# Hybrid encoder block: depthwise convolution for even and odd tokens at once, its input and the gated product through memory

## The chip, the cores and the metric

The kernel runs on the 8 cores of one Trainium2 chip, one program on each with its own tokens. The time is device microseconds of the slowest core, the median of several runs.

## The reference

What one core computes, for 16,384 tokens of width 1024 in five sequences (one of 8192 tokens, four of 2048), in float32:

```python
h = rmsnorm(x, norm_g) * (1 + scale) + shift      # adaLN, per sequence
a_in, a_b, a_c, a_z, b_v, b_g, b_z = split(h @ w_in, 7 * [512])
y_a = a_b * dwconv3(a_c * a_in) * silu(a_z)
u   = b_v * sigmoid(b_g)
u   = dwconv31(u) + conv_b_b                       # per channel, centred, zero padding
y_b = silu(head_layernorm(u, ln_g, ln_b)) * silu(b_z)   # norm over groups of 64 channels
out = rmsnorm(x + gate * (concat(y_a, y_b) @ w_out), final_g)
```

## The kernel before, in words

Tokens go in 32 tiles of 512. Weights and activations of the matmuls are bfloat16, channels lie in partitions, tokens along the free dimension. One iteration i of the loop at L757 holds work of three tiles, in the order in which PE gets it:

- projections of tile i (`mm1`, matmuls at L521, blocks of 8 over the 1024 inputs): the GLU (`glu`, 64 matmuls, writes `u`), `t1_group` (64), `b2_b` (32, writes `gb`), `b2_a` (64, writes `ga`), 224 in all;
- `conv_phase` for tile i-1: the 31-tap convolution of `u` on PE (`conv_b`), with the head layer norm started in between;
- `stage_d` for tile i-2: 64 matmuls with `w_out`, the residual add (L714, DVE), square (L666, ACT), reciprocal root (L673, POOL), scaling (L678, DVE), store (L681).

The convolution reads the tile `X`, in which the 128 partitions are 4 taps x 32 channels: copies of `u`, each shifted by one token, made by `x_fill` (L587), 16 transfers from SBUF to SBUF. The weights `WC` are diagonal 128 x 32 blocks. Each of the 4 banks of 128 channels takes 8 steps `q` of 4 taps for 4 column strips `g` of 32 channels that run side by side in PE's array:

```python
bank[32 * g:32 * g + 32, :], lhsT=WC[:, j, g, q, :], rhs=X[:, j, g, 4 * q:4 * q + NT],
```

So there are 128 matmuls of 512 columns per tile at L595. Before each of them stands its weight load (PEld).

Layer norm of bank j: ACT copies the bank (L600), PE subtracts the group mean (`ln_center`, L605), ACT squares (L607), PE averages the squares (`ln_var`, L613), ACT takes Ln and Exp (L620, L622), DVE multiplies (L623); a whole iteration later ACT applies Silu (L630, `ln_out`) and POOL multiplies by `gb` into `yT` (L633). `conv_phase` puts centering and variance matmuls between the four convolutions; what is left goes as hooks behind the first three half banks of `stage_d`.

PSUM is eight banks of 512 columns, handed out by least recent use (`PB`, L247). The four convolution banks stay held until `ln_out`, so `stage_d` turns over four others. The row buffers `xb` are six (`XB`, L245). Every engine works off its instructions in the order written; a wait is in front of the instruction that needs it, and all that is behind it waits too. DMAs are issued by SP: at the start of an iteration the rows of tile i+1 (`a_load`, L308), after the GLU `x_fill`, after `t1_group` the transposes of the normalised rows (L331), then the rows for the residual (`d_loads`, L646), and the stores. POOL issues the loads of `w_in`. At the first tile of a sequence `fold_gate` multiplies `w_out` by the gate, in `X` and other tiles as staging (POOL, L473).

## Time and profile before

| | |
|---|---|
| median of 3 runs | 2375.08 us (2374.8 to 2375.59) |
| profiled execution, its own time | 2376.0 us |
| span of its slowest core (first to last instruction) | 2373.2 us |
| spans of the 8 cores | 2369.6 to 2373.2 us |
| mean granted TensorE clock | 0.990 to 0.997 of full |
| PE busy | 2322.2 us |
| DMA through the hardware queue | 340.49 MB, 53.1% of 16 engines' span |

The profile is of one execution on one core. The page gives busy time by engine, the chain of work that ended last, and groups of instructions by line. The trace behind it answers for shorter stretches: the chain of waits in order of time, the timeline of one engine, the busy time of all engines in chosen windows. A line number is one of the kernel before. A start is in us from the first instruction; in the timeline, brackets behind a row tell how long the engine had been idle before it and what released it.

### The profile page before, as it was taken

How to read it: one execution, taken by the hardware profiler on the slowest of the kernel's cores; microseconds unless marked ns; L12 is line 12 of the kernel's file. 1: busy time of each engine (PE TensorE's matmuls, PEld its weight loads, DVE VectorE, ACT ScalarE, POOL GpSimd, SP SyncE). 2: the span in 40 equal slices, each digit the busy share in tenths (PEclk: the TensorE clock that was granted, in tenths of full speed). 3: DMA queues.
4: the chain of work that ended last, by engine and by line, in shares of the span. 5: the costliest groups of instructions: out<-in, count | busy, mean ns of one | idle time of the engine just before them, and what ended most of it. 6: DMA issues, size and time to landing. Idle time of an engine off the chain costs nothing.

```text
span 2373.2 us, 42556 instructions; the slowest of 8 cores (2369.6 to 2373.2 us)
## 1 busy us (share of the span) xinstructions
PE 2322.2 (98%) x13766; PEld 1030.4 (43%) x13766; DVE 1225.3 (52%) x1967; ACT 1056.8 (45%) x1794; POOL 563.0 (24%) x514
## 2 busy tenths in 40 slices
PE   5999999999999999999999999999999999999997
PEld 1444444444444444444444444444444444444442
DVE  0245554554554555544555644555544554545547
ACT  1244345444354444354444354444454444454444
POOL 5114221211221211221211521215221242223203
PEclk9999999999999999999999999999999999999998
DMA  9945654445554445655446745456645655646444
GB/s 236 218 109 155 162 131 140 130 113 136 162 128 143 125 111 143 162 127 144 126 109 179 207 125 146 119 163 177 162 120 142 172 142 153 162 118 204 110 128 170
DMA packets 274565, 350.54 MB, mean 148 GB/s; under 512 B 144392, under 2 KB 217264, under 8 KB 273328
## 3 DMA queue, kind: packets, MB, share of 16 engines
q1 hardware_dynamic: 266736, 340.49, 53.1%
q0 software_dynamic: 7616, 7.34, 2.2%
q8 instruction: 118, 1.93, 0.3%
q14 instruction: 95, 0.78, 0.1%
HBM read 185.73 MB, written 67.13 MB: 107 GB/s over the span
## 4 chain that ended last, share of the span: by engine, by line
PE 96%; DMA 1%; SPq 1%; issue 1%; DVE 1%; POOL 0%; ACT 0%; POOLq 0%; DVEq 0%; ACTq 0%
PE pb L521 63%; PE pb L710 18%; PE pb L595 9%; PE pb L505 2%; PE pb L605 2%; PE pb L613 1%; DMA w_out_sb<-w_ada 1%; SPq L294 0%; DMA xb<-x 0%; SPq L349 0%; PE pb L358 0%; PE pb L486 0%; DVE xb L678 0%; POOL yT L633 0%; SPq L308 0%
## 5 line engine op out<-in xcount | busy, mean ns | idle before, releaser
L521 PE MATMUL pb<-hT,w_in_sb 128*128 128x512 bf16 x6944 | 1505.1, 379 | 0.6 <-PE pb L486 0.2
L521 PEld LDWEIGHTS pb<-hT,w_in_sb 128*128 128x128 bf16 x6944 | 679.3, 98 | 820.9 <-issue 3.1
L710 PE MATMUL pb<-w_out_sb,yT 128*128 128x512 bf16 x2048 | 462.0, 382 | 3.8 <-POOL yT L633 3.4
L673 POOL TENSOR_TENSOR rsE<-msE,mhalf 128x1 f32<-128x1 f32 x128 | 70.1, 548 | 1131.0 <-DVE msE L671 1128.9
L710 PEld LDWEIGHTS pb<-w_out_sb,yT 128*128 128x128 bf16 x2048 | 200.1, 98 | 246.1 <-issue 20.7
L553 DVE TENSOR_TENSOR t<-pb,tp 128x512 bf16<-128x512 f32 x128 | 88.9, 694 | 324.1 <-ACT xs L314 293.4
L576 DVE SCALAR_TENSOR_TENSOR tp<-t,caT_sb,tp 128x512 f32<-128x512 bf16 x256 | 230.1, 899 | 28.0 <-DVE tp L573 0.9
L623 DVE SCALAR_TENSOR_TENSOR pb<-pb,cbs,tp 128x512 f32<-128x512 f32 x128 | 96.8, 756 | 285.4 <-PE pb L613 216.2
L595 PE MATMUL pb<-X,WC 128*32 128x512 bf16 x4096 | 238.6, 380 | 0.0
L532 DVE SCALAR_TENSOR_TENSOR u<-tp,pb 128x512 bf16<-128x512 f32 x128 | 88.4, 691 | 273.7 <-PE pb L521 261.2
L633 POOL TENSOR_TENSOR yT<-tp,gb 128x512 bf16<-128x512 f32 x128 | 155.3, 1214 | 242.4 <-ACT tp L630 242.3
L530 ACT ACTIVATE tp<-pb 128x512 f32<-128x512 f32 x128 | 76.1, 597 | 303.5 <-PE pb L521 270.6
L559 ACT ACTIVATE tp<-pb 128x512 f32<-128x512 f32 x128 | 76.2, 597 | 303.4 <-PE pb L521 292.9
L551 ACT ACTIVATE tp<-pb 128x512 f32<-128x512 f32 x128 | 76.1, 597 | 252.4 <-PE pb L521 239.5
L714 DVE TENSOR_TENSOR xb<-pb,xb 128x512 f32<-128x512 f32 x248 | 169.8, 685 | 29.4 <-PE pb L710 25.5
L323 POOL TENSOR_SCALAR xs<-xb,rsA 128x1024 bf16<-128x1024 f32 x128 | 176.5, 1394 | 7.4 <-POOL rsA L320 5.3
L678 DVE SCALAR_TENSOR_TENSOR xb<-xb,rsE,fg_bc 128x1024 f32<-128x1024 f32 x124 | 164.7, 1328 | 5.0 <-POOL rsE L673 4.6
L666 ACT ACTIVATE tp<-xb 128x1024 bf16<-128x1024 f32 x124 | 131.1, 1057 | 70.8 <-DVE msE L671 57.2
L567 ACT ACTIVATE gb<-pb 128x512 bf16<-128x512 f32 x128 | 76.5, 598 | 179.4 <-PE pb L521 166.7
L595 PEld LDWEIGHTS pb<-X,WC 128*32 128x32 bf16 x4096 | 100.4, 96 | 125.1 <-issue 34.4
L600 ACT ACTIVATE sq<-pb 128x512 bf16<-128x512 f32 x128 | 75.8, 593 | 153.0 <-PE pb L595 150.5
L561 DVE TENSOR_TENSOR ga<-pb,tp 128x512 bf16<-128x512 f32 x128 | 87.7, 687 | 106.1 <-PE pb L521 98.0
(89 smaller groups left out, 1379.4 us busy)
## 6 DMA issues: line engine op xcount, KB each, us to landing
xb<-x SPq DMA_DIRECT2D x252, 512.0 KB, 8.2
X<-u SPq DMA_DIRECT2D x512, 135.0 KB, 2.9
y<-xb SPq DMA_DIRECT2D x124, 512.0 KB, 3.6
X<-w_out SPq DMA_DIRECT2D x20, 512.0 KB, 6.8
w_in_sb<-w_in POOLq DMA_DIRECT2D x28, 256.0 KB, 16.6
yT<-w_ada SPq DMA_DIRECT2D x6, 1024.0 KB, 10.9
w_out_sb<-w_ada SPq DMA_DIRECT2D x6, 1024.0 KB, 15.2
yT<-w_out SPq DMA_DIRECT2D x10, 512.0 KB, 7.7
```

The source lines that it names most:

```text
L323: T.op("gpsimd", lambda e, xbuf=xbuf, sub=sub: e.tensor_scalar(out=xs[:, sub, :], in0=xbuf[:], scalar1=rsA[:, sub:sub + 1], scalar2=1.0, o ...
L521: T.op("tensor", lambda e, bank=bank, kc=kc: e.matmul(bank[:], lhsT=w_in_sb[:, kc, col0:col0 + 128], rhs=hT[:, kc, :], start=(kc == 0), st ...
L532: T.op("vector", lambda e: e.scalar_tensor_tensor(out=u[:, j, 15:15 + NT], in0=th[:], scalar=1.0, in1=bank2[:], op0=ALU.add, op1=ALU.mult) ...
L553: T.op("vector", lambda e: e.tensor_tensor(out=t1[:, j, 1:1 + NT], in0=bank2[:], in1=ain[:], op=ALU.mult), reads=[akey, bkey2], writes=[(" ...
L576: T.op("vector", lambda e, k=k: e.scalar_tensor_tensor(out=acc[:], in0=t1[:, j, k:k + NT], scalar=caT[:, j * KA + k:j * KA + k + 1], in1=a ...
L595: T.op("tensor", lambda e, q=q, g=g: e.matmul(bank[32 * g:32 * g + 32, :], lhsT=WC[:, j, g, q, :], rhs=X[:, j, g, 4 * q:4 * q + NT], start ...
L623: T.op("vector", lambda e: e.scalar_tensor_tensor(out=bank[:], in0=bank[:], scalar=cbs[:, j:j + 1], in1=r[:], op0=ALU.add, op1=ALU.mult), ...
L633: T.op("gpsimd", lambda e: e.tensor_tensor(out=yT[:, 4 + j, :], in0=r[:], in1=gb[:, j, :], op=ALU.mult), reads=[rkey, ("gb", ti % 2, j)], ...
L666: T.op("scalar", lambda e: e.activation(out=jb[:].bitcast(BF16), in_=xbuf[:], func=AF.Square, accum_out=ssE[:, c:c + 1]), reads=xkeys, wri ...
L678: T.op("vector", lambda e: e.scalar_tensor_tensor(out=xbuf[:], in0=xbuf[:], scalar=rsE[:, c:c + 1], in1=fg_bc[:], op0=ALU.mult, op1=ALU.mult),
L710: T.op("tensor", lambda e, bank=bank, kc=kc, sub=sub, h=h: e.matmul(bank[:], lhsT=yT[:, kc, sub * 128:(sub + 1) * 128], rhs=w_out_sb[:, kc ...
L714: T.op("vector", lambda e, bank=bank, xbuf=xbuf, h=h: e.tensor_tensor(out=xbuf[:, h * NT:(h + 1) * NT], in0=bank[:], in1=xbuf[:, h * NT:(h ...
```

## The change

1. **Convolution.** `X` has 8 taps x 16 channels in its partitions, and `u` is split by parity of the token: 256 odd and 256 even ones. A weight block of 128 x 32 gives 16 channels for both parities. A matmul has 256 columns, 4 steps `q` suffice, and a bank holds two halves `hh` of 64 channels: 128 matmuls of 256 columns per tile. Columns of a bank that has channels x parity in partitions are tokens of one half, so bias and scale of squares, normalisation and Silu differ by half, and each of these becomes two instructions of 256 columns.
2. **Order.** `conv_phase` runs the four convolutions in one piece. Centerings, variances and the rest of the norm are hooks behind the first five half banks of `stage_d`.
3. **Input through memory.** `x_out` writes `u` to a scratch tensor in HBM (8 transfers), `x_in` reads `X` from it (8 transfers of 16 partitions, rows of 17,400 bytes).
4. **Gated product through memory.** The bank's layout differs from that of `gb` and `yT`. So `gb` goes out (`g_out`, 4 transfers) and comes back as `gbV` (`g_in`, 1), and POOL's product goes out (`y_out`, 1) and comes back as `yT` (`y_in`, 4).
5. **x rows by ACT's queue.** `a_load` and `d_loads` are issued by ACT; rows are every other token. `a_load` comes after the GLU, the squares of the rows go from `t1_group` to `b2_b`, the transposes behind `b2_b`, `d_loads` into `b2_a`.
6. `conv_a` has five DVE instructions in place of four. The last tile's `stage_d` takes the first half of the contraction for all eight half banks first. Constant matrices are built on DVE.

The diff, cut to its core:

```diff
-NQ = 8
+NQ = 4
+HN = NT // 2
+NG = 32
+PAD = 8
+UW = HN + 2 * PAD
+XN = NG * UW - 4
...
-        WC = sb("WC", [128, 4, 4, NQ, 32], BF16)
+        WC = sb("WC", [128, NG * NQ, 16, 2], BF16)
...
-        X = sb("X", [128, 4, 4, XW], BF16)
+        X = sb("X", [128, NG, UW], BF16)
...
-        gb2 = [sb("gb%d" % i, [128, 4, NT], BF16) for i in range(2)]
+        gb = sb("gb", [128, 4, NT], BF16)
+        gbV = sb("gbV", [128, 4, NT], BF16)
+        yV = gb
...
+        def rows(t, i, sub):
+
+            return t[i * NT:(i + 1) * NT, :].rearrange("(h p t) d -> t h p d", h=2, t=2)[1 - sub // 2, sub % 2]
+
+        def a_load(i, after=(), eng="scalar"):
             for sub in range(4):
                 xbuf, xkey = XB.next(pin=True)
-                T.dma("sync", lambda e, xbuf=xbuf, r=row0 + sub * 128: e.dma_start(out=xbuf[:], in_=x_d[r:r + 128, :]),
+                T.dma(eng, lambda e, xbuf=xbuf, sub=sub: e.dma_start(out=xbuf[:], in_=rows(x_d, i, sub)),
...
+        def g_out(i):
+
+            dst = gd[i % 2].rearrange("(c t) (j hh n) -> hh t c j n", t=2, j=4, hh=2)
+            T.dma_batch("sync", [lambda e, hh=hh, t=t: e.dma_start(out=dst[hh, t], in_=gb[64 * hh:64 * hh + 64, :, t * HN:(t + 1) * HN])
+                                 for hh in range(2) for t in range(2)], [("gb", j) for j in range(4)], [("gd", i % 2)], "st_g")
...
+        def y_out(i):
+            T.dma("sync", lambda e: e.dma_start(out=yd[i % 2], in_=yV[:].rearrange("p j n -> p (j n)")),
+                  reads=[("gb", j) for j in range(4)], writes=[("yd", i % 2)], semkey="st_y")
...
+        def x_out(i):
+
+            dst = ud[i % 2].rearrange("h c (j g l) -> h j g c l", j=4, g=8)
+            T.dma_batch("sync", [lambda e, h=h, j=j: e.dma_start(out=dst[h, j], in_=u_sb[i % 2][:, j, h, :]) for h in range(2) for j in range(4)],
+                        [("u", i % 2)], [("ud", i % 2)], "st_u")
...
+        def x_in(i):
+
+            Xf = X[:].rearrange("p g l -> p (g l)")
+            T.dma_batch("sync", [lambda e, w=w: e.dma_start(out=Xf[16 * w:16 * w + 16, 0:XN], in_=ud[i % 2, w % 2, :, (w + 1) // 2:(w + 1) // 2 + XN])
+                                 for w in range(8)], [("ud", i % 2)], Xkeys, "xfill")
 
         def conv_b(j):
             bank, bkey = PB.next(pin=True)
-            for q in range(NQ):
-                for g in range(4):
-                    T.op("tensor", lambda e, q=q, g=g: e.matmul(
-                        bank[32 * g:32 * g + 32, :], lhsT=WC[:, j, g, q, :], rhs=X[:, j, g, 4 * q:4 * q + NT],
-                        start=(q == 0), stop=(q == NQ - 1), tile_position=(0, 32 * g)),
-                        reads=[("WC", j)] + Xkeys, writes=[bkey], signal=(q == NQ - 1 and g == 3))
+            for hh in range(2):
+                for q in range(NQ):
+                    for g in range(4):
+                        G = 8 * j + 4 * hh + g
+                        T.op("tensor", lambda e, q=q, g=g, G=G, hh=hh: e.matmul(
+                            bank[32 * g:32 * g + 32, hh * HN:(hh + 1) * HN], lhsT=WC[:, G * NQ + q].rearrange("p c t -> p (c t)"),
+                            rhs=X[:, G, 4 * q:4 * q + HN], start=(hh == 0 and q == 0), stop=(hh == 1 and q == NQ - 1), tile_position=(0, 32 * g)),
+                            reads=["WC0", "WC1"] + Xkeys, writes=[bkey], signal=(hh == 1 and q == NQ - 1 and g == 3))
...
-            T.op("vector", lambda e: e.scalar_tensor_tensor(out=bank[:], in0=bank[:], scalar=cbs[:, j:j + 1], in1=r[:], op0=ALU.add, op1=ALU.mult),
-                 reads=[rkey, "cbs"], writes=[c["bkey"]])
+            for hh in range(2):
+                k, sl = 2 * j + hh, slice(hh * HN, (hh + 1) * HN)
+                T.op("vector", lambda e, k=k, sl=sl: e.scalar_tensor_tensor(out=bank[:, sl], in0=bank[:, sl], scalar=cbs[:, k:k + 1], in1=r[:, sl],
+                                                                            op0=ALU.add, op1=ALU.mult),
+                     reads=[rkey, "cbs"], writes=[c["bkey"]])
...
+            first = [half(n // 2, n % 2, (0, 1, 2, 3)) for n in range(8)] if i == ntiles - 1 else None
...
+            cs = [conv_b(j) for j in range(4)]
+
+            def norm(*steps):
+                def f():
+                    for fn, j in steps:
+                        fn(cs[j])
+                    if (ln_rstd, 3) in steps:
+                        table_of(AF.Silu, 1)
+                return f
+
             table_of(AF.Ln, 0)
...
+            return {0: norm((ln_center, 0), (ln_center, 1)),
+                    1: norm((ln_center, 2), (ln_var, 0), (ln_rstd, 0)),
+                    2: norm((ln_center, 3), (ln_var, 1), (ln_rstd, 1)),
+                    3: norm((ln_var, 2), (ln_rstd, 2)),
+                    4: norm((ln_var, 3), (ln_rstd, 3))}, (k, cs)
...
-            if 1 <= i < ntiles - 1:
-                a_load(i + 1)
...
+            if cur_ok:
+                u_halo(i)
+            if 1 <= i < ntiles:
+                x_out(i - 1)
+            if left is not None:
+                y_out(i - 2)
+            if 1 <= i < ntiles:
+                x_in(i - 1)
+            if left is not None:
+                y_in(i - 2)
             left = None
...
+            if 1 <= i <= ntiles:
+                g_in(i - 1)
+            if 1 <= i < ntiles - 1:
+                a_load(i + 1)
...
+                if i + 1 < ntiles:
+                    a_square(i + 1, j)
+            if cur_ok:
+                g_out(i)
+            if i + 1 < ntiles:
+                a_scale(i + 1)
+                if i > 0:
+                    a_transpose(i + 1)
...
+                if j == 2 and 2 <= i <= ntiles:
+                    d_loads(i - 2)
```

## Rows read from the trace of the kernel before

**Rows 1.** The page: header, and busy time of each engine with its share of the span.

```profile
span 2373.2 us, 42556 instructions; the slowest of 8 cores (2369.6 to 2373.2 us)
PE 2322.2 (98%) x13766; PEld 1030.4 (43%) x13766; DVE 1225.3 (52%) x1967; ACT 1056.8 (45%) x1794; POOL 563.0 (24%) x514
```

**Rows 2.** The chain that ended last: share by engine (page); its longest early piece.

```profile
PE 96%; DMA 1%; SPq 1%; issue 1%; DVE 1%; POOL 0%; ACT 0%; POOLq 0%; DVEq 0%; ACTq 0%
...
23.44 17.76 DMA w_out_sb<-w_ada
```

**Rows 3.** Chain of waits, one steady tile: start us, us, engine and line, instructions.

```profile
385.31 48.35 PE pb L521 x224
433.66 3.57 PE pb L595 x64
437.23 0.32 PE pb L605
...
444.03 0.22 PE pb L605
...
446.41 10.36 PE pb L710 x48
456.77 0.43 PE pb L521 x2
```

**Rows 4.** Windows of that tile: convolution, output, projection stage; busy us, instructions.

```profile
core 3: us, PE busy (x) PEld busy (x) DVE busy (x) ACT busy (x) POOL busy (x), PEclk, DMA share, GB/s
433.65:442.30 8.65, 8.65 (x135) 3.60 (x135) 3.27 (x9) 4.68 (x8) 0.00 (x0) 1.00 0.01 2
442.30:456.78 14.48, 14.48 (x69) 6.50 (x67) 9.61 (x15) 10.90 (x19) 1.09 (x2) 1.00 0.09 37
385.31:433.66 48.35, 48.35 (x229) 21.79 (x230) 25.00 (x38) 17.41 (x30) 12.31 (x11) 1.00 0.73 188
```

**Rows 5.** Windows: a stretch of the transposes of 128 columns.

```profile
100.95:101.34 0.39, 0.39 (x10) 0.39 (x8) 0.39 (x2) 0.00 (x0) 0.00 (x0) 1.00 1.06 305
```

**Rows 6.** Windows: centering after a wait, then the convolution's first instructions.

```profile
2319.81:2320.11 0.30, 0.30 (x1) 0.07 (x1) 0.00 (x0) 0.23 (x1) 0.30 (x2) 1.00 0.77 314
2320.11:2320.14 0.03, 0.03 (x5) 0.03 (x8) 0.00 (x0) 0.00 (x0) 0.03 (x1) 1.00 1.17 482
```

**Rows 7.** Groups by line: ACT and DVE of the layer norm and residual; busy, mean ns.

```profile
L607 ACT ACTIVATE sq<-pb,cbs 128x512 bf16<-128x512 f32 x128 | 87.4, 683 | 1.5 <-PE pb L613 0.3 <-PE pb L605 0.3
L600 ACT ACTIVATE sq<-pb 128x512 bf16<-128x512 f32 x128 | 75.8, 593 | 153.0 <-PE pb L595 150.5 <-PE pb L605 2.5
L622 ACT ACTIVATE tp<-tp 128x512 f32<-128x512 f32 x128 | 80.7, 630 | 11.7
L637 ACT ACT_TABLE_LOAD x64 | 82.1, 1283 | 1.1
L666 ACT ACTIVATE tp<-xb 128x1024 bf16<-128x1024 f32 x124 | 131.1, 1057 | 70.8 <-DVE msE L671 57.2 <-DVE xb L714 12.7
L714 DVE TENSOR_TENSOR xb<-pb,xb 128x512 f32<-128x512 f32 x248 | 169.8, 685 | 29.4 <-PE pb L710 25.5 <-DMA xb<-x 0.8
L623 DVE SCALAR_TENSOR_TENSOR pb<-pb,cbs,tp 128x512 f32<-128x512 f32 x128 | 96.8, 756 | 285.4 <-PE pb L613 216.2 <-ACT tp L622 69.2
```

**Rows 8.** SP's issues: timeline of the tile, landing (page), issue ns min/median/max (by line).

```profile
400.50 10.47 SPq L587 DMA_DIRECT2D X<-u  x16
...
xb<-x SPq DMA_DIRECT2D x252, 512.0 KB, 8.2
X<-u SPq DMA_DIRECT2D x512, 135.0 KB, 2.9
...
L646 SPq DMA_DIRECT2D xb<-x x124: 327/391/1673, 208.4 to 2325.1; - x124
```

**Rows 9.** The end: chain of waits, and PE's timeline with the idle time before it.

```profile
2323.23 7.64 DMA xb<-x
...
2331.80 0.38 PE L613 MATMUL pb<-sq,Bm 128*128 128x512 bf16 x1 [2.98 <-DVE xb L714]
```

More of the change, by code:

```diff
@@ L579, in conv_a @@
[L579 to L589 removed]
+            out, okey = TP.next()
@@ L703, in stage_d, with half @@
             yT = yT2[i % 2]
-            row0 = i * NT
+            def half(sub, h, kcs, bk=None):
+                bank, bkey = bk or PB.next(pin=kcs[-1] != 7)
+                for kc in kcs:
+                    T.op("tensor", lambda e, kc=kc: e.matmul(
+                        bank[:], lhsT=yT[:, kc, sub * 128:(sub + 1) * 128], rhs=w_out_sb[:, kc, h * NT:(h + 1) * NT],
+                        start=(kc == 0), stop=(kc == 7)),
+                        reads=[("yT", i % 2, kc), ("w_out", kc)], writes=[bkey], signal=(kc == kcs[-1]))
+                return bank, bkey
+            first = [half(n // 2, n % 2, (0, 1, 2, 3)) for n in range(8)] if i == ntiles - 1 else None
             for sub in range(4):
@@ L707, in stage_d @@
                 for h in range(2):
-                    bank, bkey = PB.next()
-                    for kc in range(8):
-                        T.op("tensor", lambda e, bank=bank, kc=kc, sub=sub, h=h: e.matmul(
-                            bank[:], lhsT=yT[:, kc, sub * 128:(sub + 1) * 128], rhs=w_out_sb[:, kc, h * NT:(h + 1) * NT],
-                            start=(kc == 0), stop=(kc == 7)),
-                            reads=[("yT", i % 2, kc), ("w_out", kc)], writes=[bkey], signal=(kc == 7))
+                    bank, bkey = half(sub, h, (0, 1, 2, 3, 4, 5, 6, 7)) if first is None else half(sub, h, (4, 5, 6, 7), first[sub * 2 + h])
                     T.op("vector", lambda e, bank=bank, xbuf=xbuf, h=h: e.tensor_tensor(
@@ L784, in build_nc @@
                 if ntiles > 1:
-                    a_load(1, [("w_in", 2, 7)])
+                    a_load(1, [("w_in", 2, 7)], "sync")
                 gate_loads([("w_in", 3, 7)])
@@ L823, in build_nc, with also @@
             if i == ntiles - 1:
-                x_fill(i)
+                x_out(i)
+                x_in(i)
             if i == ntiles:
-                hooks[1] = lambda f=hooks.get(1): (f(), conv_a(ntiles - 1, 2))
-                for j in range(4):
-                    hooks[3 + j] = lambda j=j: (ln_out(left[0], left[1][j]), conv_a(ntiles - 1, 3) if j == 1 else None)
+                def also(n, *fns):
+                    old = hooks.get(n, lambda: None)
+                    hooks[n] = lambda: [f() for f in (old,) + fns]
+                also(1, lambda: conv_a(ntiles - 1, 2))
+                also(3, lambda: conv_a(ntiles - 1, 3))
+                also(5, lambda: ln_out(left[0], left[1][0]), lambda: ln_out(left[0], left[1][1]))
+                also(6, lambda: ln_out(left[0], left[1][2]), lambda: ln_out(left[0], left[1][3]), lambda: y_out(ntiles - 1), lambda: y_in(ntiles - 1))
             if i >= 2:
```

261 lines of the change are left out of this document (118 added, 143 removed).

## The prediction

> **What bounds the kernel now.** I read the page first: PE is busy for 98% of the span, DVE, ACT and POOL for half of it or less [rows 1], and the chain that ended last is PE for 96% [rows 2]. So only what shortens or stalls PE's stream counts. The chain of waits over one steady tile shows that stream [rows 3]: it starts at 385.31 and again at 456.77, a period of 71.46 us, made of 224 projection matmuls (48.35), four convolutions of 32 matmuls, and 64 output matmuls with the layer-norm matmuls of 0.22 between them. There is no stall. The windows give 8.65 for the convolution stage, with three centerings and two variances in it, and 14.48 for the output stage with the other three [rows 4]. 30 such tiles have all stages.
>
> **The change, part by part.** Sums are against the profiled execution's own 2376.0 us (span 2373.2); the median of the three runs is 0.9 lower, so a gain is taken off 2375.1.
>
> *Convolution matmuls.* Still 128 per tile, in 32 rounds of four column strips, but with 256 columns in place of 512. Today a round takes 0.2159 (48.35/224 for one 512-column matmul; two convolutions, 16 rounds, take 3.57 with their switch) [rows 3]. Transposes of 128 columns run back to back: 7 weight loads begin in 0.39 (an eighth was in flight), 0.0556 a pair [rows 5]. On the line through both, 256 columns cost 0.109. So 32 rounds go from 6.91 to 3.49: 3.42 less per tile, if instructions come fast enough. That is the first unknown. A pair of weight load and matmul would have to issue each 27 ns; now it issues each 55.8 (3.57/64) [rows 3]. Ends: 27 ns (the array's own pace) and 55.8 (nothing gained). The nearest row is for the first: after PE had waited for ACT, 0.30 passed with only the centering matmul, and then 8 loads and 4 matmuls (a fifth, the centering, was in flight) began within 0.03 us [rows 6]. They had piled up while the array was busy with one matmul and a switch, so the queue can be ahead of the array. I take 3.49. The Trainium skill, "TensorE: Matmul & The Clock Gate", section Back-to-back issue gap, speaks against this: it gives about 81 ns per matmul of 128 columns in a stream of loads and matmuls. By it 128 pairs would take over 10 us and the change would lose; the transposes at 0.0556 with their loads contradict it here.
>
> *Mode switches.* A 128-row by 32-column convolution next to a full-array matmul costs extra: the centering in front of one takes 0.32 where it takes 0.22 in the output stage [rows 3], so 0.10 each. Today there are six edges per tile, afterwards two, all LN matmuls having moved into the output stage: 0.40 less.
>
> *Layer-norm order.* The eight matmuls stay (1.73). But their ACT work (four copies, table load, squares, Ln, Exp) now falls into 3.6 + 15.5 us instead of 8.65 + 14.5, and the squares, the DVE normalisation and the Silu are split in halves. Instruction cost: a 256-column half saves less than half; a 1024-column square takes 1.057 us and a 512-column copy 0.593 [rows 7], so some 0.91 ns a column and 0.13 us fixed. Eight more ACT instructions: about 1 us, where ACT is busy 33 of 71 [rows 4]. I worked through the stage with durations of [rows 7], from the first convolution matmul as 0. Copies end at 4.4, table load and its dummy at 5.9, squares 0 and 1 at 7.3, square 2 at 8.6, Ln and Exp of 0 at 10.0; the residual's square of sub 0 goes in front of hook 2's work and ends at 11.1; square 3 at 11.8; Exp of 1 at 13.2. DVE serves in order: normalisation 1 waits until 13.2, and behind it the residual add of bank 3 ends at 14.8. PE wants that bank again for its sixth half at 14.0. So a stall of 0.9 us per tile, new. Ends: 0 (if pipelining on ACT hides 0.9) and 2.
>
> *New period:* 48.35 + 3.49 + 0.10 + 13.82 + 1.73 + 0.9 = 68.4, that is 3.06 less. Times 30: 92.
>
> *Input of the convolution through memory.* The slot: x_fill starts at 400.50, the convolution at 433.66, so 33.2 us. Today 16 transfers take 10.47 to issue and 2.9 to land [rows 8]. Afterwards: 8 out (8 x 10.47/16 = 5.2, + 2.9), then 8 in. If these eight run at today's rate, 10.5 + 2.9: 21.5 in all. If at half the rate, since each lands in 16 partitions and today's in 32, 20.9 + 2.9: 31.9. Both fit, and I charge 0. Without the cover of the projections the whole 21.5 would show.
>
> *Gate and product through memory.* g_out, g_in, y_out, y_in: 10 more issues on SP, 8 x 0.65 + 2 x 0.39, 6.0 us, none in a hurry: y_in is needed in the output stage 33 us after the GLU. SP loses 8 loads of 0.39 and 8 net fill issues become 16 shorter ones: in balance it stays under half busy. Its order matters: x_in stands behind y_out, which waits for POOL's last product; POOL is busy 13.4 of 71 [rows 4], so that costs under 2 us of the slot's slack. In the five tiles that fold the gate POOL's w_out products come in between; slack again covers it. The DMA transposes move behind b2_b and end about when DVE starts hT; slack there is some 5 us, as PE has four banks free.
>
> *x rows by ACT's queue.* 8 issues of 0.39 [rows 8]: 3.1 us of ACT, in the projection stage where ACT is 17.4 of 48.35 busy [rows 4]. Their buffers were stored a stage earlier, so ACT should not wait. Queued behind them are the copies that free PE's banks, with eight banks in rotation: 0. The rows' squares move to b2_b: 1.06 + 0.59 per 1.73 of PE, so ACT keeps up, barely; 0.
>
> *conv_a:* one more DVE instruction each, 4 x 0.17; DVE is half busy: 0. *Setup* on DVE in place of POOL: hidden behind the 17.8 us in which PE's first work waits for weights [rows 2]: 0.
>
> *Tail.* In the last but one round today PE idles 2.98 for the residual rows, whose load hangs on a store, 7.64 [rows 9]. That chain does not shrink, so the last convolution's 3.4 is lost (I counted 30 tiles for it). Now ACT itself sits in that wait, with the convolution copies behind it; and the product's two trips to memory (about 3 each, the landing time in [rows 8]) are half covered by the 32 matmuls taken first (6.9). Ends 0 and 10; I take +4.
>
> Sum: 2375.1 - 92 + 4 = **2287**.
>
> **Rivals.**
> *No stall in the output stage.* ACT has 10.9 of 14.48 today without any [rows 4], and my 0.9 hangs on an order of 0.1 us steps. Then 30 x 3.96 = 119: 2375 - 119 + 0 to 4 = 2256 to 2260.
> *Issue-bound, slower.* Number of pairs is unchanged; if PE's sequencer can't deliver a pair faster than 55.8 ns, the convolution stays at 7.1, the switches give 0.4, the stall stays: 72.0 per tile, +0.6 x 30 + 4 = 2397. Place: PE, second half of each convolution stage. It decides from 51 ns a pair (6.5 us). Against it: [rows 6]. Values between give between.
> *The round trip comes late, slower.* At half rate it uses 31.9 of 33.2. If the four transfers of x rows (landing 8.2 [rows 8]) get served ahead of it, it lands 6.9 late: 75.3 per tile, +3.8 x 30 + 4: 2493. The kernel is slower than now from 2.9 us late on. Against: those rows are issued 8 us ahead of x_in. The Trainium skill, "SBUF — State Buffer", section Door 1: The DMA port swizzle, has 16 partitions at 104 GB/s and 32 at 189, which is the half rate; by that alone 2.2 MB take 21 us and the slot still holds. No row here shows 16 partitions; the 32-partition transfers, 2.2 MB in 10.47, some 210 GB/s [rows 8], agree with its second figure.
> *The stage stalls by 2 us* (ACT a little slower than its rows): 2320. *Effect lost:* if both unknowns go half wrong, 2350 or no change.
>
> **How the numbers follow.** Forecast 0.46 (own range 2272 to 2303); no stall 0.18; stall of 2 us 0.12; issue-bound 0.10, of which half slower; round trip late 0.12, of which 0.08 slower; no change 0.02. Range 2254 to 2325 holds the first three and the milder halves of the next: 0.8. A measurement here tells 0.2% from nothing. Slower 0.13, same 0.03, faster 0.84.
>
> **What would show it.** PE: 128 convolution matmuls in 3.5 to 3.6 us, one piece; output stage 15.5 plus about 0.9 of idle before its sixth half, released by the DVE add. Period 68.4. DVE normalisations waiting for ACT's Exp. SP or DMA should not release a convolution; if they do, the round trip was late. Wrong if: pairs at over 40 ns; idle in front of the convolution; ACT held by x rows ahead of t1 or of the convolution's copies; the tail over 10 us longer.

## The result, and the profile after

The changed kernel takes **2683.91 us** (median of 4 runs, 2676.06 to 2713.25) against 2375.18 for the kernel before on the same chip: ratio **1.129**, 95% interval 1.1266 to 1.1308. Forecast were 2287, range 2254 to 2325. Differences between cores and stretches of a granted clock near 0.8 occur in these runs; the tiles compared below stand at 1.00 but for what is shown.

The page of the changed kernel: header and PE's busy time, the chain by engine, the hardware queues (q1 is SP's, q10 ACT's: packets, MB, share of 16 engines), the group of DVE instructions that read the transposed rows (busy, mean ns, idle before, releaser), and three times from issue to landing.

```profile
span 2675.9 us, 43720 instructions; the slowest of 8 cores (2639.8 to 2675.9 us)
PE 2342.2 (88%) x13766; PEld 1070.8 (40%) x13766; DVE 1296.9 (48%) x2228; ACT 1141.7 (43%) x2050; POOL 540.6 (20%) x496
q1 hardware_dynamic: 279728, 298.06, 54.6%
q10 hardware_dynamic: 35136, 127.94, 13.7%
PE 39%; SPq 36%; DMA 11%; DVE 5%; issue 4%; ACT 2%; POOL 1%; DVEq 0%; ACTq 0%; POOLq 0%
L494 DVE TENSOR_SCALAR hT<-hraw,gsT,shT 128x512 bf16<-128x512 bf16 x240 | 80.2, 408 | 419.6 <-DMA hraw<-xs 419.6
X<-u_scratch SPq DMA_DIRECT2D x256, 271.9 KB, 11.5
gbV<-g_scratch SPq DMA_DIRECT2D x32, 512.0 KB, 18.5
yT<-y_scratch SPq DMA_DIRECT2D x128, 128.0 KB, 17.4
```

PE was 98% busy and 96% of the chain [rows 1, 2]; now SP's queue with the DMAs is 47% of the chain, and DVE waits 419.6 us for the transposes of the next tile's rows. It waited for none before. PE's timeline of one tile (start, us; in brackets the idle time before the row):

```profile
572.64 48.51 PE L521 MATMUL pb<-hT,w_in_sb 128*128 128x512 bf16 x224
621.08 3.68 PE L641 MATMUL pb<-X,WC 128*32 128x256 bf16 x128
...
640.05 0.59 PE L662 MATMUL pb<-sq,Bm 128*128 128x512 bf16 x1 [8.93 <-DVE xb L768]
640.74 3.45 PE L757 MATMUL pb<-w_out_sb,yT 128*128 128x512 bf16 x8
...
651.36 3.83 PE L521 MATMUL pb<-hT,w_in_sb 128*128 128x512 bf16 x17
```

The period is 78.7 us (572.64 to 651.36) in place of 71.46. The convolution does what was forecast, 128 matmuls in 3.6 us and then the output stage; in this tile nothing waits in front of it. The loss is a hole of 8.93 us after the third half bank of the output stage. It is put down to DVE's residual add (L768), but in the chain of waits DVE had been standing in front of `hT` (L494), ahead of that add in its queue:

```profile
620.00 8.38 SPq L332
...
633.11 3.21 DMA hraw<-xs
...
637.07 2.03 DVE hT L494 x6
639.09 0.61 DVE xb L768
...
640.05 0.60 PE pb L662
```

SP's timeline of the same tile shows why the rows were late:

```profile
588.16 6.21 SPq L624 DMA_DIRECT2D u_scratch<-u  x8
594.53 0.77 SPq L558 DMA_DIRECT2D y_scratch<-gb  x1
599.59 3.56 SPq L632 DMA_DIRECT2D X<-u_scratch  x8
603.25 2.60 SPq L564 DMA_DIRECT2D yT<-y_scratch  x4
606.03 4.78 SPq L554 DMA_DIRECT2D gbV<-g_scratch  x1
610.91 8.93 SPq L550 DMA_DIRECT2D g_scratch<-gb  x4
620.00 14.37 SPq L332 DMA_TRANSPOSE hraw<-xs  x4
```

The queue runs from the end of the GLU to 634.37 with one gap, the landing of `u_scratch`. Where an issue stretches (`gbV` 4.78 where it took 0.33 in a tile of e6 below, the transposes 14.37 where they took 5.66 before), DMAs asked for earlier have not landed yet; that this is the reason is inferred. Windows of the tile, with DMA share and GB/s as the last two numbers and the granted clock ahead of them:

```profile
588.16:636.42 48.26, 42.96 (x310) 20.86 (x308) 19.41 (x33) 19.01 (x34) 6.17 (x5) 0.97 0.99 212
609.00:617.00 8.00, 8.00 (x39) 3.63 (x37) 5.86 (x8) 1.26 (x3) 6.17 (x5) 1.00 0.99 120
630.00:640.00 10.00, 1.12 (x6) 0.29 (x3) 3.48 (x10) 1.49 (x3) 0.00 (x0) 0.68 0.73 107
640.00:644.00 4.00, 3.85 (x9) 1.27 (x10) 2.00 (x5) 3.10 (x6) 0.00 (x0) 0.51 0.00 0
644.00:646.20 2.20, 2.20 (x12) 0.99 (x11) 1.88 (x5) 1.61 (x3) 0.34 (x1) 1.00 0.03 7
```

From the GLU to the first `hT` (48.26 us) the engines are 99% busy, yet in the middle they move only 120 GB/s: that is `x_in`. Then they have next to nothing to do for the rest of the tile. And the hole costs more than itself: the granted clock is 0.68 in mean while PE idles and 0.51, its lower level of 1.2 GHz, in the 4 us behind, so the 8 matmuls there take 3.45 in place of 1.89; from 644 on it is 1.00 again.

### The profile page after: what moved, and what is told of

The parts are those of the page before. It is cut to its first block, busy times and chain, and to the rows that moved or that the text cites. A ratio compares the mean times of both kernels' runs of the same rounds, so it can differ in the third digit from the quotient of the medians.

```text
span 2675.9 us, 43720 instructions; the slowest of 8 cores (2639.8 to 2675.9 us)
## 1 busy us (share of the span) xinstructions
PE 2342.2 (88%) x13766; PEld 1070.8 (40%) x13766; DVE 1296.9 (48%) x2228; ACT 1141.7 (43%) x2050; POOL 540.6 (20%) x496
## 4 chain that ended last, share of the span: by engine, by line
PE 39%; SPq 36%; DMA 11%; DVE 5%; issue 4%; ACT 2%; POOL 1%; DVEq 0%; ACTq 0%; POOLq 0%
PE pb L521 25%; SPq L332 14%; PE pb L757 12%; SPq L550 11%; DMA u_scratch<-u 4%; SPq L624 4%; DMA hraw<-xs 4%; DVE hT L494 3%; SPq L632 2%; SPq L554 2%; SPq L564 2%; DMA w_in_sb<-w_in 1%; PE pb L662 1%; ACT tp L683 1%; DVE xb L768 1%
## 5 line engine op out<-in xcount | busy, mean ns | idle before, releaser
L521 PE MATMUL pb<-hT,w_in_sb 128*128 128x512 bf16 x6944 | 1549.2, 387 | 0.6 <-PE pb L486 0.2
L757 PE MATMUL pb<-w_out_sb,yT 128*128 128x512 bf16 x2048 | 541.3, 418 | 33.1 <-DMA yT<-y_scratch 19.1
L494 DVE TENSOR_SCALAR hT<-hraw,gsT,shT 128x512 bf16<-128x512 bf16 x240 | 80.2, 408 | 419.6 <-DMA hraw<-xs 419.6
L662 PE MATMUL pb<-sq,Bm 128*128 128x512 bf16 x128 | 59.2, 462 | 206.6 <-DVE xb L768 201.5
L686 POOL TENSOR_TENSOR gb<-tp,gbV 128x512 bf16<-128x512 f32 x128 | 154.2, 1206 | 232.3 <-ACT tp L683 232.3
L768 DVE TENSOR_TENSOR xb<-pb,xb 128x512 f32<-128x512 f32 x248 | 169.2, 684 | 30.7 <-PE pb L757 26.4
L615 DVE SCALAR_TENSOR_TENSOR tp<-t,caT_sb,tp 128x256 f32<-128x256 bf16 x256 | 161.4, 630 | 34.4 <-DMA gate_scratch<-tp 6.9
L641 PE MATMUL pb<-X,WC 128*32 128x256 bf16 x4096 | 131.0, 287 | 45.9 <-issue 27.5
L674 DVE SCALAR_TENSOR_TENSOR pb<-pb,cbs,tp 128x256 f32<-128x256 f32 x256 | 125.6, 491 | 85.9 <-ACT tp L671 71.8
L321 POOL TENSOR_TENSOR rsA<-msA,mhalf 128x4 f32<-128x4 f32 x32 | 32.6, 1018 | 662.7 <-DVE msA L319 662.7
L683 ACT ACTIVATE tp<-pb,lnb_sb,lng_sb 128x256 f32<-128x256 f32 x256 | 143.2, 561 | 12.0
```

The lines of the kernel that those rows point to most:

```text
L494: T.op("vector", lambda e, kc=kc: e.tensor_scalar(out=hT[:, kc, :], in0=hraw[:, kc, :], scalar1=gsT[:, kc, s:s + 1], scalar2=shT[:, kc, s: ...
L521: T.op("tensor", lambda e, bank=bank, kc=kc: e.matmul(bank[:], lhsT=w_in_sb[:, kc, col0:col0 + 128], rhs=hT[:, kc, :], start=(kc == 0), st ...
L615: T.op("vector", lambda e, h=h: e.scalar_tensor_tensor(out=out[:, h * HN:(h + 1) * HN], in0=t1[:, j, 1 + h * HN:1 + (h + 1) * HN], scalar= ...
L641: T.op("tensor", lambda e, q=q, g=g, G=G, hh=hh: e.matmul(bank[32 * g:32 * g + 32, hh * HN:(hh + 1) * HN], lhsT=WC[:, G * NQ + q].rearrang ...
L683: T.op("scalar", lambda e, k=k, sl=sl: e.activation(out=r[:, sl], in_=bank[:, sl], func=AF.Silu, scale=lng[:, k:k + 1], bias=lnb[:, k:k + 1]),
L686: T.op("gpsimd", lambda e: e.tensor_tensor(out=yV[:, j, :], in0=r[:], in1=gbV[:, j, :], op=ALU.mult), reads=[rkey, "gbV"], writes=[("gb", j)])
```

## The experiments

Two theories at first, of why the transposes are late. **Q**: the order on SP's queue; they stand behind issues that are held up by `x_in`. **V**: the volume; what is asked for between the GLU and `hT` needs more engine time than there is. Then **M**: the later squares and transposes (part 5) by themselves. **R**: the 256-byte packets of the transposes share the engines with rows asked for by ACT's queue and starve. All ratios are against the kernel before in runs beside it.

**The order alone (e1).**

```diff
-            if cur_ok:
-                g_out(i)
             if i + 1 < ntiles:
                 a_scale(i + 1)
                 if i > 0:
                     a_transpose(i + 1)
+            if cur_ok:
+                g_out(i)
```

> The changed kernel with one line moved: the four g_out transfers are issued behind the four transposes. Theory Q (the 16-partition rows of x_in hold SP's rings for some 18 us; what stands behind them on SP, the transposes last, lands late, DVE waits for hT with the residual adds behind it, and PE runs out of banks): the transposes are issued some 8 us earlier, hT is ready about when the convolution ends, and most of PE's 9 us stall in the output stage goes: 2350 to 2450 us, period 69 to 72. Theory V (the DMA engines have too much to move in this stretch in whatever order): 2600 to 2680. Theory M (the transposes are too late because their rows were squared behind b2_b): 2600 to 2680 as well.

Measured 2697.5, ratio 1.139 [1.127, 1.151]: nothing gained. Order alone is not it. In a tile of its trace the four transposes are asked for from 660.02 on, ahead of the gate, and still land only at 674.6 to 682.6: `gbV`, in front of them on SP's queue, lands at 670.1, and ACT's rows for the residual, asked for from 665.7 on, at 680.3.

**Wider targets for `x_in` (e2), and both (e3).** Two shifts that lie in neighbouring partitions are read by one transfer: 5 transfers, three of them into 32 partitions. For it `x_out` writes to the other parity's place.

```diff
-e.dma_start(out=Xf[16 * w:16 * w + 16, 0:XN], in_=ud[i % 2, w % 2, :, (w + 1) // 2:(w + 1) // 2 + XN])
-                                 for w in range(8)
+e.dma_start(out=Xf[max(0, 32 * k - 16):min(128, 32 * k + 16), 0:XN],
+            in_=both[max(0, 16 - 32 * k):min(32, 144 - 32 * k), k:k + XN])
+                                 for k in range(5)
```

> The changed kernel, but x_in has five transfers, three of them into 32 partitions, in place of eight into 16 (the two parities change places in the scratch tensor); same bytes, same values. Theory Q with the rate set by how many partitions a transfer reaches: a 17,400-byte row goes from 2.27 us to some 1.2 us in the three wide transfers, x_in holds the rings for some 12 us instead of 18, the transposes move forward by as much and the stall shrinks by 5 to 7 us per tile: 2450 to 2550 us. If long rows as such are slow, or by theory V: 2650 to 2690. Theory M: no change either.

> Both edits. Theory Q: no stall before the third half bank is left; what remains is my forecast of the period, 67.5 to 69.5: 2260 to 2330 us. Theory V: over 2500. Theory M: over 2600.

e2: 2649.1, ratio 1.114 [1.112, 1.117]. e3: 2549.1, 1.073 [1.064, 1.082]. e2 misses Q's range and is 1 us under that of V and M; e3 misses those of Q and M and is in V's. Alone the wider targets give 35 us and the order nothing; together 135. So there is more than one limit, and each hides the other.

**Part 5 alone, on the kernel before (e4).** x rows by ACT's queue, squares in `b2_b`, transposes behind them, `d_loads` in `b2_a`; the convolution and its fills as before.

> The kernel before with part 5 alone: x rows issued by ACT, a_load behind the GLU, squares of the rows in b2_b, transposes behind b2_b, d_loads in b2_a. No memory trips, convolution as before. Theory Q: its rings are free, so the later transposes still land in time: 2375 within 0.5%. Theory M: the transposes land late by themselves, period some 9 us longer: 2600 us or more.

Measured 2397.2, ratio 1.008 [1.005, 1.011]. SP's timeline, the transposes' time from issue to landing and the list of waits, all of core 3:

```profile
570.34 7.18 SPq L331 DMA_TRANSPOSE hraw<-xs  x4
...
DMA to landing us min/median/max: 3.0/3.3/15.0
...
DVE hT L494 <- DMA hraw<-xs: 188.2, 29, 9.4
```

DVE now waits 6.5 us per tile (188.2/29; it waited for none before), and PE notices little: on the slowest core 13 of the 29 periods after the first stay at 71.5, the others go up to 73.5. So the slack behind the transposes is some 6 us, as the prediction had it, and M falls: part 5 costs 22 us, not 300. But it uses that slack up. Why, the transposes show one by one. On the slowest core the first three of a tile land in a median of 3.3 to 3.4 us and the fourth in 12.5 (up to 15.0); before, all four took 3.3. The fourth is mostly asked for 0.1 us behind the first of the residual rows, which ACT's queue now carries. Nothing of the round trips is in this kernel.

**x rows asked for earlier.** e5 is e3 with `a_load` at the start of the iteration, by SP (where the kernel before has it); e7 is the changed kernel with that edit alone.

```diff
+            if 1 <= i < ntiles - 1:
+                a_load(i + 1, (), "sync")
             for j in range(4):
                 if cur_ok:
                     glu(i, j)
...
-            if 1 <= i < ntiles - 1:
-                a_load(i + 1)
```

> e3_both, with the rows of the next tile (a_load) issued by SP at the start of the iteration, as in the kernel before, in place of by ACT behind the GLU. Theory V (volume: between the end of the GLU and the transposed rows the 16 DMA engines are busy all the time, and their work in that stretch is longer than PE's): 2 MB leave the full stretch for one in which the engines idle, 5 to 8 us of engine time, and the stall shrinks by as much: 2330 to 2420 us. Theory Q (only the order behind x_in on SP's queue matters): no change from e3_both, 2520 to 2560.

> The changed kernel with a_load alone moved back to the start of the iteration, on SP. Theory V: the stall shrinks by 5 to 8 us per tile: 2440 to 2560 us. Theory Q: 2660 to 2700, since x_in and all behind it are as before.

e5: **2412.1**, ratio 1.013 [1.008, 1.017], the best version of the change that was found, and in V's range. e7: 2695.4, 1.131 [1.124, 1.139], a miss for V and in Q's range. Two megabytes less stand in the stretch, and it is as long as ever. Its trace, a window of 46 us from the GLU, and SP's issues of the gate and the first two transposes:

```profile
684.56:731.00 46.44, 43.36 (x303) 20.99 (x306) 19.39 (x32) 17.92 (x33) 6.17 (x5) 0.96 0.98 167
...
704.52 7.60 SPq L550 DMA_DIRECT2D g_scratch<-gb  x4
712.28 14.25 SPq L332 DMA_TRANSPOSE hraw<-xs  x2
```

The share of busy engines is 0.98 as before, at 167 GB/s in place of 212. In the changed kernel the x rows landed at 596.3, beside the way out of `u` and ahead of `x_in`. Without them `x_in` starts 7.5 us behind the GLU in place of 11.4, but the last transpose lands 49.7 us behind it in place of 48.2: the first is asked for at 712.28 and lands at 731.2, just behind the residual rows of ACT's queue (730.8). The busy share is no sum of work either: 0.98 to 0.99 stand beside 120, 167 and 212 GB/s. In a tile of e5 that is not late, by contrast (windows; PE's and SP's timelines):

```profile
623.50:656.43 32.93, 32.93 (x155) 14.79 (x153) 18.44 (x31) 11.30 (x20) 6.17 (x5) 1.00 0.90 185
633.50:641.50 8.00, 8.00 (x39) 3.64 (x38) 4.80 (x10) 4.31 (x8) 0.00 (x0) 1.00 0.94 189
...
656.43 3.68 PE L643 MATMUL pb<-X,WC 128*32 128x256 bf16 x128
...
671.86 5.34 PE L759 MATMUL pb<-w_out_sb,yT 128*128 128x512 bf16 x24 [1.07 <-DVE msE L722]
677.04 3.19 PE L521 MATMUL pb<-hT,w_in_sb 128*128 128x512 bf16 x14
...
647.38 5.47 SPq L332 DMA_TRANSPOSE hraw<-xs  x4
```

`x_in` goes at 189 GB/s, the transposes are issued in 5.47, the last issue ends 3.6 us ahead of the convolution and lands 1.3 us ahead of it, and the period (607.99 to 677.04) is 69.05.

**`x_in` left out (e6).** The changed kernel, `X` read in 7 of the 32 tiles only; the others convolve an old `X`.

```diff
-            if 1 <= i < ntiles:
+            if i == 1 or (1 <= i < ntiles and fold is not None):
                 x_in(i - 1)
```

> The changed kernel, but x_in is issued only for the first tile, for the five tiles after a fold and for the last one, 7 of 32; the other tiles convolve what is left in X (the convolution of those tiles is left out as a result, its instructions all run). Theory V: some 17 us of engine time per tile leave the stretch, the stall goes in 25 tiles, and what remains is the period I forecast, 67.5 to 68.4, with 6 tiles at some 80: 2320 to 2370 us. If the two trips of the gate and the product, or the later squares, were what makes the transposes late: over 2500.

Measured 2429.4, ratio 1.018 [1.009, 1.027]. By the starts of its convolution stages, 16 of the 30 periods are 69.0 to 69.3 us, and those of tiles that still read `X` are some 80 (79.8, 79.6, 80.2, 80.4, 80.5). So `x_in` is what the loss cannot do without: with it gone all other trips, the order and part 5 may stay as they are. The expectation was too low because of those tiles and the tail (below).

**`x_in` kept, the gate's and the product's trips left out (e11).** The gate is moved in two tiles, the product in 11 (11 issues of `y_scratch<-gb` in place of 32); the others multiply by an old gate and keep an old second half of `yT`.

```diff
+            trips = i <= 3 or fold is not None or tile_first[i - 3]
-            if left is not None:
+            if left is not None and trips:
                 y_out(i - 2)
...
-            if 1 <= i <= ntiles:
+            if 1 <= i <= 2:
                 g_in(i - 1)
...
-            if cur_ok:
+            if cur_ok and i <= 1:
                 g_out(i)
```

> The changed kernel; the gate's trip through memory is made in the first two tiles only, the product's in 12 of the 32, so that most tiles multiply by an old gate and their second half of y is an old one. All else, x_in of 8 transfers into 16 partitions included, stays. Leaving x_in out of 25 tiles brought their period from 79 to 69.1 us. If any DMA work that goes helps in proportion (theory V), this takes 4 to 7 of the 54 us of engine work of a tile and with them the same from the lateness of 9.6: periods of 72 to 76 where nothing is left of the trips, 2450 to 2600. If it is x_in's own rows that hold the transposes up, whatever else is asked for (theory P), nothing is gained but the queue's 3 to 9 us in front of the transposes: 2600 to 2690.

Measured 2567.3, ratio 1.079 [1.072, 1.086], median period 76.5: 117 us gained where e6 gained 255. This is in V's range: the trips of gate and product, left out together, count, and `x_in` counts for more.

**e5 without its order (e10).** Wider targets and early x rows, the gate's way out ahead of the transposes again.

> The kernel of e5 without its swap: the gate's way out is issued ahead of the transposes again. Theory V (the volume of DMA work between the end of the GLU and the need for the transposed rows decides, the order on SP does not): 2400 to 2440, as e5. Theory Q (an issue that is held up in front of the transposes decides): the gate's issues take 8.9 us in the changed kernel and 3.0 in e5; if they still stretch, the transposes start 6 us later, with 9 us of slack ahead of the convolution and the DVE work behind it, and most tiles come late: 2480 to 2650.

Measured 2524.9, ratio 1.059 [1.055, 1.063]. The order that was worth nothing in e1 is worth 113 us here. But not as Q has it: the issues of the gate don't stretch (3.01 and 2.54). The transposes take 13.18 in one tile and 6.44 in the next, and PE idles 2.55 and 4.31 us in these tiles, so how long they are held at the issue doesn't tell how late they land. In the second of these tiles the last one is asked for 0.04 us behind the first of the residual rows (1124.42) and takes 14.5 us to land:

```profile
1042.87 3.01 SPq L550 DMA_DIRECT2D g_scratch<-gb  x4
1046.81 13.18 SPq L332 DMA_TRANSPOSE hraw<-xs  x4
...
1115.34 2.54 SPq L550 DMA_DIRECT2D g_scratch<-gb  x4
1119.28 6.44 SPq L332 DMA_TRANSPOSE hraw<-xs  x4
```

**One transfer for three pairs (e9).** e5 with `X` read in 3 transfers, the middle one into 96 partitions:

```diff
+            mid = bass.AP(tensor=m0.tensor, offset=m0.offset, ap=[[1, 3], [NG * UW, 32], [1, XN]])
+            e.dma_start(out=Xf[16:112, 0:XN], in_=mid)
```

> The kernel of e5 (transposes ahead of the gate's way out, pairs of shifts in one transfer, x rows requested at the start of the iteration), with X read back in 3 transfers instead of 5: the three pairs become one transfer into 96 partitions, the two ends stay at 16 partitions. Same bytes, same rows of 17,400 bytes. What the engines need for such a row was 2.27 us when each transfer landed in 16 partitions and 1.36 us when three of five landed in 32. If the target's number of partitions sets that, a row now needs under 1.2 us, a tile some 2 us less engine work, and fewer tiles are late: 2340 to 2400 against e5's 2412. If the row's length or the memory sets it, 1.36 stays and so does the time: 2400 to 2425. If 16 engines now write into the few partitions of one neighbourhood again, rows get slower and the time passes 2430.

Measured 3165.7, ratio 1.323 [1.320, 1.326]. The time passes 2430, as the third answer has it, but not for its reason. While this transfer runs, the window shows

```profile
1068.00:1083.00 15.00, 14.95 (x70) 6.77 (x70) 11.48 (x17) 7.48 (x14) 6.18 (x5) 1.00 0.23 62
```

0.23 of 16 engines, 3 to 4, and 62 GB/s; PE idles 17.6 to 29.4 us in front of each convolution but the first, waiting for `X`. The source's outermost dimension is 3. The Trainium skill, "DMA: Bandwidth & Descriptors", section Why a DMA increments its semaphore by 16 and not by 1, has the engines of a transfer as the largest number up to 16 that divides the slowest dimension of both sides, so 3; the row agrees. e12, which put the split of the residual rows on top of e9, has the same fault and tells nothing of that split:

> The kernel of e9 with the four residual rows' transfers on ACT's queue split: two are requested in the first of the b2_b groups, some 12 us earlier, two stay where they are. Now all four (2.1 MB) run beside the transposes. Theory R (transposes share the 16 engines packet by packet with what ACT's queue asks for, 256 bytes against 4096, and starve): fewer late tiles, 15 to 50 us less than e9. Theory V without R: the volume in front of the transposes grows by 1 MB, no gain or up to 30 us worse than e9.

Measured 3124.6.

**What is left in e5.** On the profiled core its 31 convolution stages span 63.5 us more than 61.6 (the first, shorter period) + 29 x 69.1. Three tries at it. e14: two of the four residual rows' transfers are asked for in the first `b2_b`.

> The kernel of e5 (x_in as five transfers) with the four transfers of residual rows on ACT's queue split: two are requested at the first of the b2_b groups, some 20 us before the convolution, two stay 4 us before it. In e5 all four come while the transposes are on their way. Theory R (256-byte packets of the transposes share the engines packet by packet with ACT's 4096-byte rows and starve): of e5's late tiles (periods of 70.6 to 77 in place of 69.1, 60 us in all) a third or more goes, 2365 to 2395. Theory V alone: 1 MB more stands in front of the transposes, as much goes behind them: 2405 to 2440.

Measured 2409.4, ratio 1.014 [1.011, 1.016], as e5. The gain that R expected is not there, but R does not fall with it: with two of the residual rows' transfers now in front of all four transposes, these land in medians of 7.6, 9.7, 7.1 and 7.3 us, where e5 has 4.4, 4.1, 3.3 and 8.8. e16: squares back among the `t1` groups and transposes behind them, as the kernel before has it; e17 is e16 with e14's split.

> The kernel of e5 with the squares of the x rows back among the t1 groups and the transposes behind them, where the kernel before has them: they are asked for 17 us before the convolution instead of 9. If what is left in e5 is lateness of the transposes (60 us of periods over 69.1 on the profiled core, a tail of 19 more than before, and some 10 us in the first tile), 8 us more of slack takes most of the 60: 2340 to 2375, faster than the kernel before or equal to it. If the DMA work in front (x_in, gate, product) has not ended by then in any case (theory V in its strict form: the transposes land when the volume is through, whenever asked), little is gained: 2390 to 2415. Rows of ACT that wait for x rows not yet landed would show as late t1 groups and cost more.

> e16 with the residual rows' transfers split as in e14. e14 gained nothing over e5 (2409 against 2412), so within 10 us of e16 either way; if two of the four transfers now run beside the earlier transposes, up to 20 us more than e16.

Measured 2450.6 (1.031 [1.026, 1.037]) and 2434.6 (1.024 [1.021, 1.027]): worse than e5, e16 outside both of its ranges and e17 16 us under it where at most 10 were expected. SP's timeline of e16, with the convolution at 883.7:

```profile
867.01 14.01 SPq L332 DMA_TRANSPOSE hraw<-xs  x4
881.12 6.30 SPq L550 DMA_DIRECT2D g_scratch<-gb  x4
```

Asked for 8 us earlier they are in the midst of `x_in`, take 14.0 us to issue in place of 5.5, and the last is issued 2.6 us ahead of the convolution where it was 3.6 in e5; DVE waits longer for them (table below). The last one, at 879.5, comes 0.6 us behind the first of ACT's residual rows and lands after 12.3 us, 8.1 us behind the convolution's start. Asking for them earlier, in the midst of `x_in`, is not the cure.

What is left can be read from e5's trace. The four transposes of a late tile (period 75.1) and the four residual rows on ACT's queue:

```profile
L332 SPq DMA_TRANSPOSE hraw<-xs x4: 1216/1268/2153, 1558.8 to 1563.9; - x4
DMA to landing us min/median/max: 3.2/4.5/14.8
...
L697 ACTq DMA_DIRECT2D xb<-x x4: 334/400/858, 1564.0 to 1565.4; - x4
```

Three land in 3.2 to 4.8 us; the last, asked for 0.04 us ahead of the rows, takes 14.8. It is so on all eight cores. Their timelines have 232 tiles with both kinds of transfer. In 142 of them the last transpose is asked for 0.06 us or more ahead of the first residual row, and 8 of these have a period over 69.5. In the other 90 it is asked for later than that, and 87 of them are late; they hold 418 of the 427 us by which the periods exceed 69.1. So what is left in e5 is what R described: transposes that meet the residual rows. That is read from when things happen; no run asks for the residual rows behind the transposes. If that took the 63.5 us away and cost nothing else, e5 would come to some 2350, under the kernel before (an estimate from these rows).

**The output stage's order alone, on the kernel before (e8).** The four convolutions of 512 columns in one piece, centerings and variances as hooks.

> The kernel before with the layer-norm order of the changed one: four convolutions in one piece, centerings and variances as hooks behind the first five half banks of the output stage (a fourth sq buffer for it). My forecast for that part: four mode switches of 0.10 less and a stall of 0.9 in front of the sixth half bank, period 71.9: 2385 to 2395 us. If there is no stall: period 71.06, 2360 to 2366 us.

Measured 2379.95 (12 runs), ratio 1.0006 [0.998, 1.003]: no difference, and between the two expectations. PE's timeline:

```profile
438.99 7.09 PE L595 MATMUL pb<-X,WC 128*32 128x512 bf16 x128
...
456.86 5.34 PE L710 MATMUL pb<-w_out_sb,yT 128*128 128x512 bf16 x24 [0.31 <-DVE msE L671]
...
510.47 7.09 PE L595 MATMUL pb<-X,WC 128*32 128x512 bf16 x128
```

The period stays at 71.5: the 0.4 of saved switches is given back in a stall of 0.31 and a little more, in front of the sixth half bank, where the prediction had it.

**The tail (e15).** e14 with the last two tiles' product moved by ACT's queue instead of SP's.

> The kernel of e14 with the product's way through memory of the last two tiles requested by ACT's queue. In e5 the product's way out waits on SP behind four stores of y and lands after 10.5 us, the way in takes 5.5 more, and PE is idle for it; the last convolution's end to the last matmul is 92 us against 73 in the kernel before. If SP's order and ring are what makes the tail long, 6 to 12 us less than e14. If the two trips cost that much on any queue, the same as e14.

Measured 2416.5, ratio 1.015 [1.011, 1.020]: no gain. Of the chains of waits at the end, the trips of e5 and of e15:

```profile
2322.78 10.50 DMA y_scratch<-gb
...
2335.28 3.06 DMA yT<-y_scratch
```

```profile
2336.86 6.32 DMA y_scratch<-gb
2345.99 8.64 DMA yT<-y_scratch
```

In e14 they took 10.36 and 3.66. The way out got shorter, the way in more than that longer. The trips cost that on either queue.

## Why the prediction was wrong, step by step

| kernel | time, us | DVE waits for transposes (profiled core), us |
|---|---|---|
| kernel before, e8, e6 | 2375, 2380, 2429 | 0, 0, 119 |
| e4 | 2397 | 202 |
| e5, e14, e15 | 2412, 2409, 2417 | 148, 207, 207 |
| e16, e17 | 2451, 2435 | 225, 215 |
| e10 | 2525 | 277 |
| e3, e11 | 2549, 2567 | 314, 312 |
| e2, e7, changed kernel, e1 | 2649, 2695, 2684, 2698 | 410, 428, 420, 413 |
| e9 (its convolutions wait for `X` as well) | 3166 | 877 |

*The step that failed* is "the DMA transposes move behind b2_b and end about when DVE starts hT; slack there is some 5 us", with the zeros that were charged for the round trip of `X`, for the trips of gate and product and for the x rows on ACT's queue. What the runs showed: the last transpose lands 15 us behind the start of the convolution, DVE waits for it and PE for DVE, 8.93 us in the tile above. The slack was right (e4: 6). But each trip was held against its own deadline, and none against the transposes that are asked for behind all of them. SP, forecast under half busy, spends 41 of the 78.7 us on the seven groups of issues shown above. And nothing was said of what the residual rows on ACT's queue do to transposes on SP's beside them.

A budget would have warned. The stretch from the fill to the convolution is 33.16 us [rows 3, 8], and the window over it in the kernel before has a DMA share of 0.69: 22.9 us of engine time. `X` at the forecast's half rate takes 20.9 where it took 10.5, the x rows come into the stretch with some 8 [rows 8], the trips of gate and product with 2 MB, at 200 GB/s another 10: 22.9 - 10.5 + 20.9 + 8 + 10 = 51 in 33. That is an end 18 us late, 12 after the slack, and the forecast would have been worse than the kernel before. Measured: 48.26 us at 0.99, the hole 8.93. This is an estimate made afterwards, and its closeness is in part luck: it leaves out the way out of `u` (5.2 in the prediction), and e7 shows that the terms don't simply add, as 2 MB less made the stretch no shorter.

*How the trips make them late* is more than one limit, as the pairs of runs show. Early x rows alone give nothing (e7), wider targets alone 35 (e2), order alone nothing (e1). With wider targets in place the order gives 100 (e2 to e3) or 113 (e10 to e5), and early x rows 124 (e2 to e10) or 137 (e3 to e5); order and early rows together without wider targets were not run. As the chain of waits has it, in the changed kernel SP's queue is the bound, with `x_in` at 120 GB/s in its midst. The landings add a second part: transposes that land before the residual rows are asked for take some 3.3 us (e4, e6), those asked for while these rows are on their way 7 to 15 (e4) and 9 to 18 (e5). The rows are asked for some 4 us ahead of the convolution in e5 and the changed kernel alike, so by this reading what moves the transposes up pays in full only once it brings them ahead of that point; in e1 and e7 it does not. That `x_in` is needed for the loss is shown (e6, e2 to e3); that these two parts are the whole of it is argued, not shown.

*Round trip of `X` late*, the rival that stood for a slower result: it happened in six of 32 tiles and is small. In the tile above the 8 transfers land one after the other, the last after 17.6 us at 620.36: 32.2 us for the round trip, where the forecast had 31.9, and 0.7 us ahead of the convolution. Five other convolutions wait 0.6 to 4.1 us for `X` and the very last 10.2, 17.8 us in all. The forecast's half rate was right: 120 GB/s against 189 with three quarters of the rows in transfers of 32 partitions. The Trainium skill, "SBUF — State Buffer", section Door 1: The DMA port swizzle, has 104 and 189 GB/s for 16 and 32 partitions; the rows agree roughly. The slow rate took its toll elsewhere.

*Convolution matmuls*: right. Forecast 3.49 + 0.10, measured 3.60 (656.43 to 660.03), 28 ns a pair. The rival of issue-bound pairs falls. So does, for matmuls of four column strips, the 81 ns per matmul of 128 columns that the Trainium skill, "TensorE: Matmul & The Clock Gate", has in its section Back-to-back issue gap.

*Mode switches and the stall*: place right, size 0.6 short. From the convolution's start to the next projections a tile of e5 takes 20.61 (656.43 to 677.04); forecast 20.04. Idle before the sixth half bank are 1.07 and some 0.4 in smaller pieces, against 0.9. So the new period is 69.05 to 69.1, forecast 68.4. Where nothing is late, the idea gives 2.4 us per tile.

*Tail*: forecast +4. From the start of the 31st of the 32 convolutions to the last matmul the kernel before takes 72.8 us (2291.7 to 2364.5), e5 91.9, the changed kernel 95.6: 19 to 23 more. The product's trips were to cost 3 each way, half covered. In e5 they cost 10.50 and 3.06, then 2.63 and 3.38, with two batches of four issues between them, and are covered by nothing.

*The sum for the changed kernel.* From the first convolution to the 31st, 163.7 to 2569.7 = 2406 us, against 61.6 + 29 x 69.1 = 2065 without lateness: 341. Of these some 42 are not lateness: four periods of 89.6 to 91.3 in place of 79.6 (the median), in which the granted clock is 0.81 while PE is busy (from 810 to 880 us, for one); why, no run shows, and two of the cores have no such period. Period 0.6 to 0.7 over forecast: 20. Tail: 19. First convolution 4.7 later (163.7 against 159.0): 5. Together 385 of the 397 us between forecast and measurement. The tail holds the 10.2 us of the last convolution's wait for `X`.

## What to carry to other kernels

A stage that is off the critical path has one budget for all its DMAs: write down everything asked for between two points, on all queues, with the slowest rate among them, and hold it against what is requested last, not each transfer against its own use. Then look at each transfer's landing, and not only at the engines' busy share: it shows which other transfers it met. Here 2.4 us of PE time per tile were bought with a queue that had PE wait 9 us for its last requests; the better versions (e5, e14) still lose some 1.3%. When two limits lie close together, ablations of one at a time can show nothing: test them in pairs. And a run that moves half of a rival's cause to another place (e14) doesn't refute the rival.

## What was not expected of the hardware

- Rows of 17,400 bytes went at 120 GB/s into 16 partitions at a time (8 transfers), and at 189 with three of 5 transfers into 32. While the slow ones run, the engines count as busy (0.99).
- A transpose of SP's queue that is asked for while rows of ACT's queue are on their way lands in 7 to 15 us (e4) or 9 to 18 (e5) in place of 3.3.
- A source whose outermost dimension is 3 ran on 3 to 4 of 16 engines: 62 GB/s, and the kernel took 31% longer than e5.
- Transposes issued while `x_in` or the trips behind it are under way hold SP for 13 to 14 us in place of 5.5 (changed kernel, e10, e16); asking 8 us earlier brought nothing (e16).
- After 9 us of idle time PE's granted clock is 0.51 for 4 us more (1.2 GHz, the lower of its levels, in place of 2.4); it makes the 7.9 us of extra idle time cost 9.6 in the period.
